# Zero rows under the shallow matmul operands of the sample's latent attention

## The reference, cut to what matters

```python
ckv_all = jnp.concatenate([cache_b_ckv[l], ckv], axis=1)   # 256 + 16 rows, 256 wide
kpe_all = jnp.concatenate([cache_b_kpe[l], kpe], axis=1)   # 256 + 16 rows, 32 wide
kv = (ckv_all @ w_ukv[l]).reshape(b, ckv_all.shape[1], H_B, NOPE_B + V_B)
ob = mla_attention(q_nope, q_pe, kv[..., :NOPE_B], kpe_all, kv[..., NOPE_B:], pos, k_pos_b)
# inside: s = (q_nope . k_nope + q_pe . k_pe) * scale ; p = softmax(s) ; p . v
```

## Time and profile before

| | |
|---|---|
| median of 3 runs | 1946.3 us (1945.57 to 1948.06) |
| profiled execution, span from first to last instruction | 1941.1 us |
| TensorE matmuls (PE) busy | 1873.9 us, 97% |
| TensorE weight loads (PEld) busy | 1774.3 us, 91% |
| VectorE (DVE) busy | 889.1 us, 46% |
| ScalarE (ACT) busy | 532.2 us, 27% |
| GpSimd (POOL) busy | 603.8 us, 31% |
| mean granted TensorE clock | 0.993 of full speed |
| HBM traffic | 90 GB/s over the span |

### The profile page before, as it was taken

The page is one execution under the profiler, slowest core; times in us unless marked ns, Lnnn a source line. Parts: engine busy times, 40 slices in busy tenths (PEclk is TensorE's granted clock), DMA queues, the critical chain, the costliest instruction groups (busy, mean ns, idle before and its releaser), DMA issues.

```text
span 1941.1 us, 33651 instructions
## 1 busy us (share of the span) xinstructions
PE 1873.9 (97%) x12512; PEld 1774.3 (91%) x12512; DVE 889.1 (46%) x1240; ACT 532.2 (27%) x998; POOL 603.8 (31%) x246
## 2 busy tenths in 40 slices
PE   7899999999999999999999999999999999999995
PEld 6898877799999999999999888779999999999994
DVE  5464443277543134224747454425764422431357
ACT  3244344312211121112222543433122111211122
POOL 2322310033333333333433122012333333333343
PEclk9999999999999999999999999999999999999997
DMA  5223512342222222222222342134322222222223
GB/s 166 98 68 111 139 67 79 104 154 91 76 76 73 71 73 76 76 76 76 87 89 66 111 117 93 49 104 139 136 76 70 71 75 76 76 76 76 76 76 119
DMA packets 60016, 175.02 MB, mean 90 GB/s; under 512 B 7704, under 2 KB 13496, under 8 KB 59768
## 3 DMA queue, kind: packets, MB, share of 16 engines
q1 hardware_dynamic: 59928, 173.89, 27.5%
HBM read 155.22 MB, written 19.43 MB: 90 GB/s over the span
## 4 chain that ended last, share of the span: by engine, by line
PE 89%; DVE 5%; issue 2%; ACT 1%; DMA 1%; SPq 1%; POOL 0%; DVEq 0%; ACTq 0%; POOLq 0%
PE acc L1002 62%; PE acc L929 12%; PE psU L899 2%; PE acc L985 2%; PE psU L885 1%; PE psU L909 1%; DVE sum_x L1252 1%; DVE h_hi L1469 1%; PE psS L864 1%; PE psU L911 1%; PE acc L864 1%; PE acc L1075 1%; PE acc L1090 1%; DMA rel_rows<-rel_row 1%; PE psU L848 1%
## 5 line engine op out<-in xcount | busy, mean ns | idle before, releaser
L506 POOL TENSOR_TENSOR w_lo<-w_raw,w_hi 128x1024 fp32r<-128x1024 f32 x236 | 592.2, 2510 | 1317.1 <-ACT w_hi L528 1317.1
L528 ACT ACTIVATE w_hi<-w_raw 128x1024 fp32r<-128x1024 f32 x236 | 250.0, 1059 | 1060.3 <-PE acc L1002 1012.6
L1002 PE MATMUL acc<-h_hi,w_hi 128*128 128x320 f32 x1664 | 381.0, 310 | 0.5 <-DVE tmp L1373 0.5
L1002 PE MATMUL acc<-h_lo,w_hi 128*128 128x320 f32 x1664 | 379.7, 309 | 0.0
L1002 PE MATMUL acc<-h_hi,w_lo 128*128 128x320 f32 x1664 | 379.4, 309 | 0.0
L1002 PEld LDWEIGHTS acc<-h_hi,w_hi 128*128 128x128 f32 x1664 | 278.9, 188 | 1.8 <-issue 1.3
L1002 PEld LDWEIGHTS acc<-h_lo,w_hi 128*128 128x128 f32 x1664 | 278.7, 188 | 0.0
L1002 PEld LDWEIGHTS acc<-h_hi,w_lo 128*128 128x128 f32 x1664 | 278.6, 188 | 0.0
L1002 PE MATMUL acc<-act_hi,w_hi 128*128 128x320 f32 x704 | 160.5, 309 | 2.2 <-DVE act_lo L1492 2.2
L1002 PE MATMUL acc<-act_lo,w_hi 128*128 128x320 f32 x704 | 160.3, 309 | 0.0
L1002 PE MATMUL acc<-act_hi,w_lo 128*128 128x320 f32 x704 | 160.2, 309 | 0.0
(11 more groups left out here) (219 smaller groups left out, 2558.3 us busy)
## 6 DMA issues: line engine op xcount, KB each, us to landing
w_raw<-in_w SPq DMA_DIRECT2D x240, 512.0 KB, 3.3
gates<-gate SPq DMA_DIRECT2D x32, 320.0 KB, 2.2
tmp<-gates SPq DMA_DIRECT2D x32, 320.0 KB, 3.2
cb_t<-in_cb_t SPq DMA_DIRECT2D x16, 256.0 KB, 3.2
cb_v<-in_cb_v SPq DMA_DIRECT2D x16, 256.0 KB, 2.9
xT<-in_xT SPq DMA_DIRECT2D x8, 320.0 KB, 6.3
out_yT<-xT SPq DMA_DIRECT2D x8, 320.0 KB, 2.4
out_new_ckv<-ckvT SPq DMA_DIRECT2D x2, 640.0 KB, 3.9
```

The costliest lines, as they stand in the source:

```text
L506: pool.tensor_tensor(w_lo[:, s, :], w_raw[:, s, :], w_hi[:, s, :], ALU.subtract).then_inc(s_w_lo, 1)
L528: act.activation(w_hi[:, slot, :], w_raw[:, slot, :], ACT.Copy).then_inc(s_w_hi, 1)
L1002: last = pe.matmul(acc[:, m % 2, half, 0:HALF], w, x[:, half * HALF:(half + 1) * HALF], start=s0, stop=s1)
```

## The change

`cvn`, `cb_p` and `q_pe` become 128 partitions tall at the same places. The real data stay in the first 16 or 32 partitions; the others are cleared once per layer by VectorE, and the matmuls L875 and L911 read all 128. For `pT` the 112 partitions below the new keys' probabilities hold whatever was last written there, and meet zeros of `cvn`. The fill of `cvn` waits until the four groups L1107 have read `qB`, and ScalarE waits for it (`s_cvn_zero`) before its first copy. In VectorE's queue the fills stand between the prompt jobs and the first `new_columns`.

```diff
-        cvn = at("cvn", [DEC_SEQ, DEC_BATCH, KV_LORA], F32, B0)
+        cvn = at("cvn", [P, DEC_BATCH, KV_LORA], F32, B0)
-        cb_p = at("cb_p", [ROPE, 4, KEYS_B], F32, rstd_off)
+        cb_p = at("cb_p", [P, 4, KEYS_B], F32, rstd_off)
-        q_pe = at("q_pe", [ROPE, DEC_BATCH, H_B, DEC_SEQ], F32, sum_off)
+        q_pe = at("q_pe", [P, DEC_BATCH, H_B, DEC_SEQ], F32, sum_off)
...
-                    sp.dma_start(cb_p[:, s, 0:PAST], io["cb_p"][l * DEC_BATCH + b]).then_inc(bcache_loaded[s], 16)
+                    sp.dma_start(cb_p[0:ROPE, s, 0:PAST], io["cb_p"][l * DEC_BATCH + b]).then_inc(bcache_loaded[s], 16)
...
-                        act.activation(cvn[:, 2 * (r - 4):2 * (r - 3), :],
+                        if r == 4:
+                            act.wait_ge(s_cvn_zero, l + 1)
+                        act.activation(cvn[0:DEC_SEQ, 2 * (r - 4):2 * (r - 3), :],
...
-                        last = pe.matmul(out, cvn[:, b, a * P:(a + 1) * P], pT[0:DEC_SEQ, s, PAST:PAST + P],
+                        last = pe.matmul(out, cvn[:, b, a * P:(a + 1) * P], pT[:, s, PAST:PAST + P],
...
-                then(newc, dve.tensor_copy(cb_p[:, s, PAST:KEYS_B], kpeT[NOPE:QK_B, t0:t0 + DEC_SEQ]))
+                then(newc, dve.tensor_copy(cb_p[0:ROPE, s, PAST:KEYS_B], kpeT[NOPE:QK_B, t0:t0 + DEC_SEQ]))
...
-                then(qpe, dve.tensor_copy(q_pe[:, :, :, :].rearrange("p b h q -> p h b q"),
+                then(chain, dve.memset(q_pe[:, :, :, :].rearrange("p b h q -> p (b h q)"), 0.0))
+                then(qpe, dve.tensor_copy(q_pe[0:ROPE, :, :, :].rearrange("p b h q -> p h b q"),
                                           qB[r, :, SEQ:T].rearrange("p h (b q) -> p h b q", q=DEC_SEQ)))
+                for r0, r1 in ((ROPE, 2 * ROPE), (2 * ROPE, P)):
+                    then(chain, dve.memset(cb_p[r0:r1, :, :].rearrange("p s k -> p (s k)"), 0.0))
+                dve.wait_ge(s_sprep, l * 8 + 4)
+                dve.memset(cvn[:, :, :].rearrange("p b n -> p (b n)"), 0.0).then_inc(s_cvn_zero, 1)
 
                 dve.wait_ge(s_pv, l * JOBS + J_SB)
                 for b in range(3):
                     new_columns(l, b)
```

More of the change, by code:

```diff
@@ L303, in build @@
         s_spread, s_kcopy = sem("kpe_spread"), sem("odd_keys_copied")
-        s_qpe = sem("q_pe_copied")
+        s_qpe, s_cvn_zero = sem("q_pe_copied"), sem("new_values_cleared")
         s_scored, s_maxed, s_exped, s_probs = sem("scored"), sem("maxed"), sem("exped"), sem("probs_ready")
@@ L1515, in _ @@
                                              ALU.mult, ALU.mult).then_inc(s_y, 1)
-N_CHAIN = 281
+N_CHAIN = 284
 PROLOGUE_CHAIN = 2 * KD - 2
```

## The result

The changed kernel takes 1933.6 us (median of 4 runs, 1929.41 to 1936.04) where the kernel before takes 1947.2 us (median of 4, 1945.57 to 1948.8) beside it: a ratio of 0.9921, 95% interval 0.9902 to 0.9939. A second set gave 1930.5 us (5 runs) against 1947.5 us (9 runs), ratio 0.9908, interval 0.9889 to 0.9927. So it is 13.6 and 17.0 us faster by the medians. The profiled execution spans 1927.0 us, 14.1 us less than the one before.

A forecast was written before the change was run, and what follows sets the result against it. TensorE's own sequence in the attention jobs was taken as the bound. Gaps saved 18.3 us, less 1.8 for held copies and 1.0 for transfers: 15.5 us, from 1946.3 to 1930.8 us, range 1926.5 to 1936.0.

The forecast's parts named there:

- 94 gaps: TensorE's attention jobs: gaps around L875 and L911 vanish at full depth, 0.195 us each, saving 18.3 us.
- first score held: Before each layer's first score: column copies behind the cvn fill wait for GpSimd's w_lo, costing 0.9 us, 1.8 in all.
- cache transfers: Late scores: TensorE waits for cb_p's transfer after a value step, costing 0.5 us a layer, 1.0 us in all.
- Any operand under 128 rows: Cause of TensorE's gaps: they go with fewer than 128 rows, not with a small matmul; 0.19 us each way.
- the kind of the copy: VectorE's column copy, taken for the same sort as a scaling by its rate, so held by GpSimd until 338.06 us.
- the start of the fill: VectorE's cvn fill starts when L1107's fourth group is done, at 333.9 us, and takes 1.76 us.
- rival A: VectorE's column copies are not held by GpSimd, so 1.8 us come back: 1929.0 us; chance 0.27.
- 4.3 against 4.0 us: Seventh score: cb_p lands 4.3 us after the freeing value step, TensorE arrives after about 4.0 us; 0.4 us lost.
- B: Cache transfers become the pace: three scores per layer wait 1 us each, 6 us instead of 1, 1935.8 us; chance 0.14.
- C: TensorE's gaps come from something other than depth and stay, held copies cost 1.8 us: 1948.1 us; chance 0.05.
- D: Shallow TensorE passes were hidden beside deep ones and must queue at full depth: 14.4 us slower, 1960.7 us; chance 0.02.
- the 3.9 us of a job: Sign in the new profile: a job in the middle takes about 3.9 us instead of 5.03 us.

The follow-up runs named there:

- e1: The change with the score half alone (q_pe and cb_p padded, cvn and value step as before): 6.25 us less than the kernel before in the two stretches, ratio 0.9981.
- e2: The change with the value half alone (cvn padded, rotary score matmul 32 rows deep): 9.73 us less than the kernel before in the two stretches, ratio 0.9955.
- e6: The changed kernel with the first three pairs of column copies ahead of the cvn fill: first score 7.61 us behind L1109, 0.72 us sooner; program 1929.5 us.
- e9: The changed kernel's fills and waits kept, matmuls reading 32 and 16 rows as before: 8.34 and 8.33 us to first score, padding costs 1.6 us.
- e7: The changed kernel with keys of jobs 5, 6 and 7 ordered before the value-step wait: jobs 34.68 and 34.69 us per layer; program 1930.6 us.
- e3: The changed kernel with the rotary score matmul reading 64 rows and the value matmul 96: 37.84 and 37.99 us from first score to the end of the jobs.
- e5: The changed kernel again with no edit: 43.43 and 43.31 us per layer in the two stretches; program 1930.5 us.
- e8: The changed kernel with both edits, columns before the cvn fill and keys ordered early: 42.28 us per layer in the two stretches; program 1930.9 us, ratio 0.9909.

## Why the prediction was right, point by point

The median was forecast at 1930.8 us and came out at 1933.6 and 1930.5 us in the two sets; the change of the span at 15.5 us, and it was 14.1 us. The first set's median lay 6.6 us over the profiled span (1933.6 against 1927.0), where the forecast took 5.2 us from before. That a median comes within a microsecond or two of the forecast is in part chance, as the two sets of one kernel differ by 3.1 us.

| term | forecast, us | measured, us | from |
|---|---|---|---|
| 94 gaps | -18.3 | -17.6 | 2 x (3.12 + 5.67), e1 and e2 |
| first score held | +1.8 | +1.6 | 0.80 + 0.80; e6, e9 |
| cache transfers | +1.0 | +1.2 | 0.50 + 0.68, first profile against e7's sum |
| in the stretches | -15.5 | -14.8 | 7.50 + 7.31 |

1. The gaps. Mechanism and count were right, the size a little high. I took 0.195 us for all. That is what the scores show, but the value changes average 0.183 us, since the exit into the transposes costs 0.15 us. That exit was in the chain of before and I didn't price it by itself.

2. "Any operand under 128 rows" was wrong as the cause. The 96-row matmuls of the prompt in the same trace, which I did not look at, show no gap, and e3 puts the limit between 64 and 96. It did not touch the forecast, because 16, 32 and 128 lie on the right sides. It would have mattered for whoever has 96 rows and pads them. Depth is not the only cause either. The 16-column matmuls from which I argued are transposes. The prompt's L899, 128 rows deep with 64 stationary columns and no transpose, shows the same gap behind it in the kernel before:

```profile
325.35 0.85 PEld L899 LDWEIGHTS psU<-pT,vB 128*64 128x64 f32 x8 [0.93 <-ACT pT L565]
326.37 0.30 PEld L929 LDWEIGHTS acc<-h_hi,w_hi 128*128 128x128 f32 x2 [0.17 <-issue]
```

In the chain the 24 passes of L929 that follow take 3.71 us, where four times the 0.88 us of 6 passes are 3.52 us: 0.19 us. Before transposes (324.08 us) 4 passes take 0.60 us for 0.44 us. So a narrow operand can pay it too, and zero rows would not help it; no run tried zero columns.

3. The fill and the held copy. The fill was forecast at 1.76 us and took 1.76 us, the held copy is the one that was named, and GpSimd the one that held it. In both layers of all eight profiles with the fill the copy took 1.88 to 1.90 us and ended 0.04 us behind w_lo; without the fill none took over 0.19 us. The Trainium skill, "SBUF — State Buffer", Who interferes with whom, has it so for copies in the two-port mode, and the trace agrees down to a copy of 32 columns (1.89 us for 0.18). The first score lost 0.80 us, not 0.9. One weak step was the kind of the copy, taken over from a scaling because their rates agree; it held. The other was the start of the fill, and there the prediction was lucky. It had the fill start at the end of the last L1107 pass and end 0.04 us before w_lo starts (335.68 against 335.72 us), which by its own sum is a tie between the forecast and rival A. In every profile the fill started 0.50 us behind that pass (333.15 to 333.64 us here), and so it ended 0.46 us behind w_lo's start, with no doubt left for A. What the 0.50 us are made of, no run shows.

4. The transfers. 4.3 against 4.0 us gave 0.4 us for the seventh score and 0.1 for the eighth. In layer 0 the seventh's passes with their start took 0.37 us more than 0.92 (0.11 + 1.18) and the eighth's 0.14 us more (1.06 for 0.92). The term depends on the landing, which was 2.7 to 3.1 us for the keys of these two jobs in both profiles of the changed kernel, and so it moved by some tenths between layers and executions (0.5 and 0.7 us, 0.4 and 0.3 in e5).

5. The rivals. A did not happen, as the copy was held; e6 shows what it was worth, 0.72 us a layer. B did not happen, as the landings stayed near 3 us. C's cost is e9. D is excluded by e1 and e2: at full depth a pass costs 0.23 and 0.11 us, as much as it did shallow, and the shallow ones hid nothing.

6. Nothing behind the stage took a part back: from L1131 of layer 1 to the end both first profiles show 616.0 us (614.6 to 616.0 over all profiles).

7. The signs. The gaps, the 3.9 us of a job and the held copy of some 2 us came as announced. The wait before the first score was 0.83 us on the matmul side, but the row names ScalarE's copy and not cb_p's, and the seventh score's wait is named for the DMA in e5 only.

## What to carry to other kernels

Here a matmul of 16, 32 or 64 rows between matmuls of full depth cost two gaps of 0.15 to 0.19 us beside its own passes. If nothing runs beside it, pad it, or put the shallow ones together, which got 6.2 of the 17.6 us for no fill at all. Look for the same gap around operands with few columns before you call it one of depth. Before padding, look what the fills stand in front of on their engine's queue: what was done early and unseen may now come at a time when another engine holds it up. When a stage gets shorter, work out again the interval between a buffer's release and its next use; a transfer with a microsecond to spare may have none.

## What the runs showed of the hardware

The gap between depths is 0.19 us into or out of 16, 32 or 64 rows, 0.15 us from 16 rows into the transposes, and 0 at 96 rows, at a granted clock of 1.00 in these stretches. Behind full-depth matmuls of 64 columns it is 0.19 us as well, and 0.16 us into the transposes. A VectorE copy of 32 columns that started under a GpSimd subtraction ended 0.04 us behind it, for 0.18 us of its own work. A fill on VectorE that waited for TensorE's last L1109 pass started 0.50 us behind it. A float32 memset in SBUF takes 0.83 ns a column up to 2048 columns (0.91, 0.96 and 1.76 us for 1024, 1088 and 2048), with the next instruction 0.04 us behind its end. And one 512 KB weight load in layer 1, issued behind the two stores of the rotary queries (320 KB each), landed after 7.5 us in one execution of the kernel before and 8.84 us in another, and the stretch with it was 1.4 us longer in the second (893.0 and 894.5 us); over the kernels with it on the chain it took 7.8 to 8.9 us there, and in e8, where it was not, 3.5 us.
